# Gate projections of a two-layer mixer as three products of rounded parts, their sigmoids moved to a later stage

## The chip, the core and the metric

One core of a Trainium2 chip runs the whole program. The metric is device microseconds of one execution; the number given for a kernel is the median over its runs.

## What is computed

The reference is a long block on 256 tokens of width 1024. Two layers of a first block come first (feed-forward, mixer, feed-forward), then a second block with a recurrent part and 32 experts. The change touches only the mixer of the two layers. In short:

```
h      = rms_norm(x, mix_norm[l])
q,k,v  = split(h @ w_in[l])                       # four kinds of attention, a b c d
y_a .. y_d = attention of each kind               # a: 4 heads of 128, b c d: 4 heads of 64
gate   = sigmoid(h @ w_gate[l] + b_gate[l])       # 4 x 1024 columns, one block of 1024 for each branch
mixed  = sum over br of gate_br * (y_br @ w_br)   # br = a, b, c, d
x      = x + mixed @ w_out[l]
```

## The kernel before

Activations lie transposed: 8 blocks of 128 features by 256 tokens. The weights stream from HBM through a ring of three slots `RB` (`load_ring`, L388), each filled by one transfer of up to 2 MB; a slot is filled again when the step named in its job is done (for the gates the last of its four products, L353).

Most matrix products of the kernel are made of rounded parts. A weight w becomes wh, its value rounded to the format float32r by ScalarE (a Copy, `Split.high`, L417), and wl = w - wh by VectorE (`Split.low`, L426). The activations are split in the same way. A product is then the sum of three float32r products wl*xh + wh*xl + wh*xh (`mm3`, L279). The gate projections are not made so: they are plain float32 products of `HA` (the normalised x) and the raw slot (L970).

A mixer has three stages, one after the other. Every engine waits between them (`everyone`).

- `project` (L787) makes q, k, v in ten groups and at its end writes the normalised x into `HA` (L864).
- `attend` (L891) is the attention. First 12 turns of q and k on TensorE, evicted by ScalarE and VectorE in equal parts (L1036, L1100). Then one list, `attention_order()` (L159), gives the order of everything else on all three engines. Its entries are (kind, head, phase) or ("gate", h, 0) for h from 0 to 31. Each engine walks the same list and does its share of each entry.
- `branches` (L1221) makes y_br @ w_br from rounded parts, VectorE multiplies each product by its gate (L1287), GpSimd adds them up (L1308), and w_out follows.

The list begins, with one round in each line (s is a step of the top-k mask for kind d, n a step of the norm of kind a, and "c0.1" is phase 1 of head 0 of kind c):

```
c0.0 s.0 gate0
c0.1 c1.0 s.1 gate1 gate2
c0.2 c1.1 c2.0 s.2 gate3
c0.3 c1.2 c2.1 s.3 gate4
c1.3 c2.2 c3.0 s.4 gate5 gate6
c2.3 c3.1 a0.0 s.5 gate7
c3.2 a0.1 a1.0 s.6 gate8
c3.3 a0.2 a1.1 s.7 gate9 gate10
a0.3 a1.2 a2.0 s.8 gate11
a1.3 a2.1 a3.0 s.9 gate12
a2.2 a3.1 b0.0 s.10 gate13 gate14
a2.3 a3.2 b0.1 s.11 gate15
a3.3 b0.2 b1.0 s.12 gate16
...
b3.3 gate23
d0.0 n.0 gate24 gate25
d0.1 d1.0 n.1 gate26 gate27
d0.2 d1.1 d2.0 n.2 gate28 gate29
d0.3 d1.2 d2.1 gate30 gate31
d1.3 d2.2 d3.0
d2.3 d3.1
d3.2
d3.3
```

For a head of kind a, b or d: phase 0 is the logits on TensorE; phase 1 (`soften`, L1132) is on VectorE the row maxima (L1143), then the exponentials on ScalarE (L1064), then the division and mixing on VectorE (L1156 to L1170); phase 2 is three transposes on TensorE (L1004), which wait for phase 1, and their copy by ScalarE (L1070); phase 3 is the product with v (L1022) and its copy by VectorE (L1130). For kind c: phase 1 is the masked logits on VectorE (L1119), Abs, Exp and Ln on ScalarE (L1075 to L1079) and one step of VectorE (L1121); phase 2 is a product on TensorE that waits for it (L1015), an addition on VectorE (L1126) and an Exp on ScalarE (L1083); phase 3 is as above. Step n.2 has the square roots (L603), two reciprocals (L607) and four scalings (L1213).

A gate before: TensorE makes 8 float32 products of 128 x 256 (L969), and ScalarE evicts them as Sigmoid with the bias into `SG`, a part of `kept` (L1044). VectorE does nothing at a gate and walks past it.

## Time and profile before

| what | value |
|---|---|
| median of 3 runs | 2796.01 us (2793.53 to 2804.36) |
| the profiled execution: its own time | 2803.41 us |
| the profiled execution: its span | 2801.5 us |
| mean granted TensorE clock | 0.942 of full speed |
| TensorE matmul busy | 2551.5 us (91%) |
| VectorE busy | 1442.3 us (51%) |
| ScalarE busy | 1195.9 us (43%) |
| attention stage of layer 0 | 350 to 527 us of the span |
| attention stage of layer 1 | 1132 to 1308 us of the span |

The span goes from the first to the last instruction; the execution's own time adds what lies around it. PE is TensorE's matmuls and PEld its weight loads, DVE is VectorE, ACT is ScalarE, POOL is GpSimd and SPq the queue that issues the transfers. A row such as "0.71 <-DVE AT L1121" in square brackets gives the idle time of the engine just before the instruction, and what ended it. The tile names in the rows are those of the program: `AT` is the work area of the attention stage, `kept` holds q, k, v, the gates and the branch inputs, `ps` is PSUM, `mpwh`, `mpwl`, `mbwh`, `mbwl` are rounded parts of weights in the stages before and after.

### The profile page before, as it was taken

The page shows a single profiled execution, that of the slowest core. Times are in us where ns is not written, and L with a number is a line of the kernel's source. Part 1 is how long each engine was busy: PE and PEld are TensorE (multiplying, and loading weights), DVE is VectorE, ACT ScalarE, POOL GpSimd, SP SyncE. Part 2 cuts the span into 40 slices and gives each one's busy share as a digit, 9 for nine tenths or more (in the row PEclk, how much of TensorE's full clock was granted, in tenths as well). Part 3 has the DMA queues.
Part 4 walks back from the last instruction along what each step waited for, and adds up shares of the span by engine and source line. Part 5 has one row for each costly group of instructions (what it writes and reads, how often), then busy time and mean ns, then how long its engine had stood idle before and what let it go on. Part 6 is the DMA issues. An engine that isn't in the chain of part 4 may idle for free.

```text
span 2801.5 us, 52642 instructions
## 1 busy us (share of the span) xinstructions
PE 2551.5 (91%) x23295; PEld 2190.1 (78%) x23295; DVE 1442.3 (51%) x2249; ACT 1195.9 (43%) x1723; POOL 299.1 (11%) x425
## 2 busy tenths in 40 slices
PE   7999899889999999998899987787978889989997
PEld 7997788779999988787799955664467778868786
DVE  5654533566556545344665553342435442168885
ACT  5333374444344333654443452221244432157773
POOL 0100000121001000000310000531123222000000
PEclk9999999999999999999999988797979999989999
DMA  7653513347547534222466221001100002449993
GB/s 238 231 197 135 184 61 120 106 151 241 196 154 238 196 136 170 104 91 105 163 218 228 87 90 61 3 3 35 61 32 4 4 4 95 150 148 366 361 363 129
DMA packets 268885, 396.09 MB, mean 141 GB/s; under 512 B 9320, under 2 KB 172829, under 8 KB 268525
## 3 DMA queue, kind: packets, MB, share of 16 engines
q1 hardware_dynamic: 266921, 389.25, 40.6%
q8 instruction: 186, 3.05, 0.5%
q0 software_dynamic: 1120, 2.17, 0.3%
q10 hardware_dynamic: 612, 1.24, 0.1%
q14 instruction: 46, 0.38, 0.0%
HBM read 391.59 MB, written 1.05 MB: 140 GB/s over the span
## 4 chain that ended last, share of the span: by engine, by line
PE 37%; DVE 8%; DMA 5%; issue 5%; ACT 3%; POOL 2%; SPq 0%; DVEq 0%; POOLq 0%; ACTq 0%
PE ps L277 36%; DMA RB<-in_moe_w_up 5%; DVE gwl L426 2%; ACT gwh L417 1%; PE ps L499 1%; POOL H L1308 1%; DVE AR L1729 0%; POOL AR L1935 0%; POOL AR L2308 0%; DVE AR L607 0%; DVE AR L1475 0%; DVE AR L1537 0%; DVE AR L2016 0%; ACT L2514 0%; POOL AR L1471 0%
## 5 line engine op out<-in xcount | busy, mean ns | idle before, releaser
L277 PE MATMUL ps<-H,RB 128*128 128x256 f32 (+1 forms) x1712 | 454.8, 423 | 10.3 <-issue 9.1
L277 PEld LDWEIGHTS ps<-H,RB 128*128 128x128 f32 x1712 | 325.6, 193 | 124.1 <-issue 86.1
L426 DVE TENSOR_TENSOR wl<-RB,wh 128x2048 fp32r<-128x2048 f32 (+1 forms) x136 | 302.9, 2230 | 207.8 <-ACT wh L417 207.3
L277 PE MATMUL ps<-xh,wl 128*128 128x256 f32 x1408 | 402.5, 286 | 0.0
L277 PE MATMUL ps<-xl,wh 128*128 128x256 f32 x1408 | 399.2, 284 | 0.0
L277 PE MATMUL ps<-xh,wh 128*128 128x256 f32 x1408 | 399.2, 284 | 0.0
L277 PE MATMUL ps<-AR 64*64 64x64 f32 (+3 forms) x8296 | 314.6, 244 | 56.1 <-issue 18.3
L277 PEld LDWEIGHTS ps<-AR 64*64 64x64 f32 (+1 forms) x8296 | 262.5, 148 | 112.3 <-issue 82.8
L417 ACT ACTIVATE wh<-RB 128x2048 fp32r<-128x2048 f32 (+1 forms) x136 | 251.6, 1853 | 161.3 <-PE ps L277 122.9
L277 PEld LDWEIGHTS ps<-xh,wl 128*128 128x128 f32 x1408 | 271.1, 193 | 10.2 <-issue 10.1
L277 PEld LDWEIGHTS ps<-xl,wh 128*128 128x128 f32 x1408 | 271.2, 193 | 0.1
L277 PEld LDWEIGHTS ps<-xh,wh 128*128 128x128 f32 x1408 | 271.0, 192 | 0.0
L426 DVE TENSOR_TENSOR gwl<-RB,gwh 128x2048 fp32r<-128x2048 f32 x96 | 217.4, 2290 | 39.8 <-ACT gwh L417 38.9
L417 ACT ACTIVATE gwh<-RB 128x2048 fp32r<-128x2048 f32 x96 | 183.1, 1917 | 56.1 <-DMA RB<-in_moe_w_up 32.7
L277 PE MATMUL ps<-hh,wl 128*128 128x256 f32 x704 | 199.2, 283 | 0.0
L277 PE MATMUL ps<-hl,wh 128*128 128x256 f32 x704 | 199.2, 283 | 0.0
L277 PE MATMUL ps<-hh,wh 128*128 128x256 f32 x704 | 199.2, 283 | 0.0
L713 ACT ACTIVATE H<-H 128x256 f32<-128x256 f32 x88 | 36.8, 418 | 307.4 <-DVE H L740 307.4
L277 PEld LDWEIGHTS ps<-hh,wl 128*128 128x128 f32 x704 | 135.2, 192 | 0.0
L277 PEld LDWEIGHTS ps<-hl,wh 128*128 128x128 f32 x704 | 135.2, 192 | 0.0
L277 PEld LDWEIGHTS ps<-hh,wh 128*128 128x128 f32 x704 | 135.2, 192 | 0.0
L1308 POOL TENSOR_TENSOR H<-H 128x256 f32<-128x256 f32 x48 | 46.2, 1002 | 761.6 <-DVE H L1287 761.6
(415 smaller groups left out, 4522.1 us busy)
## 6 DMA issues: line engine op xcount, KB each, us to landing
RB<-in_ffn_w_gu SPq DMA_DIRECT2D x88, 1024.0 KB, 7.6
RB<-in_w_in SPq DMA_DIRECT2D x25, 2048.0 KB, 7.7
RB<-in_ffn_w_down SPq DMA_DIRECT2D x16, 2048.0 KB, 7.9
RB<-in_w_gate SPq DMA_DIRECT2D x16, 2048.0 KB, 8.8
RB<-in_moe_w_gate SPq DMA_DIRECT2D x32, 1024.0 KB, 7.6
RB<-in_moe_w_up SPq DMA_DIRECT2D x32, 1024.0 KB, 10.2
RB<-in_moe_w_down SPq DMA_DIRECT2D x32, 1024.0 KB, 8.5
RB<-in_ada_w SPq DMA_DIRECT2D x12, 2048.0 KB, 11.0
```

The lines of the kernel that those rows point to most:

```text
L277: return M.matmul(o, lhsT, rhs, start=start, stop=stop, skip_group_check=True)
L417: S.activation(self.pair(h)[0], of(slot_of(*key)), ACT.Copy).then_inc(*did("high", self.name, h))
L426: V.tensor_tensor(lo, of(slot_of(*key)), hi.bitcast(F32), ALU.subtract).then_inc(*did("low", self.name, h))
L499: ins = M.transpose(ps[0:s.shape[1], 128 * i:128 * i + s.shape[0]], s, ident[0:s.shape[0], 0:s.shape[0]])
L713: S.activation(sil[:, n % 4, 0, :], sil[:, n % 4, 0, :], ACT.Silu).then_inc(*did("silu", f, n))
L1308: P.tensor_tensor(HB[:, c, :], HB[:, c, :], tmp[:, ((br - 1) * 8 + c) % 4, :], ALU.add).then_inc(*did("merged", l, br, c))
```

## The change

The gates become products of rounded parts, like the other projections.

- ScalarE rounds the weights of a gate, 128 x 1024, into one of three buffers (two from gate 24 on, as the third lies where the last gates are written). VectorE writes the rest back in place into the ring's slot. Both are done by a new class `GateWeights`: gates 0 and 1 within `project`, gate 2 ahead of the list, and at gate h of the list, behind its eviction, the weights of gate h + 3.
- The normalised x is split as well: 8 Copies of ScalarE at the end of `project`, 8 subtractions of VectorE at the start of `attend`, ahead of its other work.
- TensorE makes 24 float32r products for a gate in place of 8 float32 ones.
- The eviction is Identity with the bias, in place of Sigmoid. The sigmoids are taken in `branches`, for a branch at once (128 x 2048, in place in `SG`).

The program's own areas move by 8 columns, and `SM` is 4 columns shorter. The transfers, their slots and what frees them stay as they were.

```diff
@@ -75,12 +75,12 @@
     pe_once="lam cum ab route ranks cw glo wide_c spread", eg="dg", ed="dd", columns="merge mgate out2 conv shift z",
     rw_in="w_in ic_in cums bon_in k_in", gdn_in="re_gate cumg wide_g kk kb_t",
     act_once="lam_exp sine f_log g_log beta group_exp expert_exp lnx_root o_root sil w2 low_act xd_high",
-    rows="k_rows v_rows rv_rows o_rows u_rows back ob b_rows k_rows_r", h_high="d_high", h_silu="d_silu",
+    rows="k_rows v_rows rv_rows o_rows u_rows back ob b_rows k_rows_r", h_high="d_high gw_high u_high", h_silu="d_silu",
     padded="shift_pad", conv_silu="z_silu", copied_a="out_a x_in_a ctx_a", part_high="m_high y_high",
-    gdn_exp="exp_c exp_d exp_g exp_tot", gdn_copy="kb_neg v_out", merge_a="yb mgated", rw_act="w_sig ic exps",
+    gdn_exp="exp_c exp_d exp_g exp_tot", gdn_copy="kb_neg v_out", merge_a="yb mgated", rw_act="opened w_sig ic exps",
     dve_once="lam_dot lam_diff nlam angle by_row dup f_in soft_f iw cq eps blk decay g_in mod scl o_square o_gated "
              "renorm_sq lnx_square a2 logits group_in expert_in combined rank known chosen cw_out cb_t xd_low",
-    copied_v="x_in ctx_v out_v vec", h_low="d_low", h_scaled="c_scaled d_scaled", part_low="m_low y_low", taps="moved",
+    copied_v="x_in ctx_v out_v vec", h_low="d_low", h_scaled="c_scaled d_scaled gw_low u_low", part_low="m_low y_low", taps="moved",
     unit_k="unit_kk kk_in", gdn_v="neg_a beta_g cumg_out qk_dec q_dec g64 d_in", pad_zero="shift_zero g2 sil_zero", gdn_mask="masked_e masked_l",
     gdn_rows="kb k_dec", inv_0="inv_own", rw_v="bt kt pr bon e1l both").items() for name in names.split()}

@@ -153,7 +153,7 @@

 BASE = 16512
 O_CST, O_RB, O_XT, O_H, O_VEC, O_SM = 0, 3912, 16200, 18248, 22344, 22728
-STAGE = 24032
+STAGE = 24024


 def attention_order():
@@ -229,8 +229,11 @@
         RB = sb("RB", O_RB, [NSLOT, 4096])
         XT = sb("XT", O_XT, [KD, T])
         H = sb("H", O_H, [2, KD * T])
+
+        RBR = sb("RBR", O_RB, [NSLOT, 4096], F32R)
+        HR = sb("HR", O_H, [2, KD, T], F32R)
         VEC = sb("VEC", O_VEC, [3, 128])
-        SM = sb("SM", O_SM, [1300])
+        SM = sb("SM", O_SM, [1296])
         HA = H[:, 0, :].rearrange("p (k n) -> p k n", k=KD)
         HB = H[:, 1, :].rearrange("p (k n) -> p k n", k=KD)
         RST = SM[:, 144:400]
@@ -780,11 +783,46 @@
             kept = sb(f"kept{l}", STAGE, [13312])
             PQK, SG = view(kept, 0, 2, NK), view(kept, 0, 32, T)
             VN, YT = view(kept, 8192, 2, 1280), view(kept, 10752, 10, T)
-            project(l, PQK, VN, view(kept, 10752, 1024))
-            attend(l, PQK, SG, VN, YT)
+            gw = GateWeights(l, [sb(f"GW{l}", STAGE + 27136, [2, 1024], F32R)[:, i] for i in range(2)]
+                             + [sb(f"GX{l}", STAGE + 7168, [1024], F32R)])
+            project(l, PQK, VN, view(kept, 10752, 1024), gw)
+            attend(l, PQK, SG, VN, YT, gw)
             branches(l, SG, YT)

-        def project(l, PQK, VN, TMP):
+        class GateWeights:
+
+
+
+            def __init__(self, l, bufs):
+                self.l, self.bufs, self.n = l, bufs, [0, 0]
+                self.of = [h % 3 if h < 24 else h % 2 for h in range(32)]
+                self.last = [max((x for x in range(h) if self.of[x] == self.of[h]), default=None) for h in range(32)]
+
+            def parts(self, h):
+                i, j = divmod(h, 4)
+                slot = job_no["gate", self.l, i] % NSLOT
+                w, lo = (x[:, slot, :].rearrange("p (k n) -> p k n", k=KD)[:, :, 128 * j:128 * j + 128] for x in (RB, RBR))
+                return self.bufs[self.of[h]].rearrange("p (k n) -> p k n", k=KD), w, lo
+
+            def high(self, upto_gate):
+                while self.n[0] < min(upto_gate, 32):
+                    h = self.n[0]
+                    hi, w, _ = self.parts(h)
+                    AC.wait_ge(*landed("gate", self.l, h // 4))
+                    if self.last[h] is not None:
+                        AC.wait_ge(*at("gate", self.l, self.last[h]))
+                    S.activation(hi, w, ACT.Copy).then_inc(*did("gw_high", self.l, h))
+                    self.n[0] += 1
+
+            def low(self, upto_gate):
+                while self.n[1] < min(upto_gate, 32):
+                    h = self.n[1]
+                    hi, w, lo = self.parts(h)
+                    DV.wait_ge(*at("gw_high", self.l, h))
+                    V.tensor_tensor(lo, w, hi.bitcast(F32), ALU.subtract).then_inc(*did("gw_low", self.l, h))
+                    self.n[1] += 1
+
+        def project(l, PQK, VN, TMP, gw):
             st, g = f"p{l}", R_MX + 8 * l
             o = STAGE + 13312
             wh, wl = sb(f"mpwh{l}", o, [2, 2048], F32R), sb(f"mpwl{l}", o + 4096, [2, 2048], F32R)
@@ -837,12 +875,17 @@
                 scaled_act(st, g, xh)
                 for gi in range(len(GROUPS)):
                     ws.high(2 * gi + 3)
+                    if gi == len(GROUPS) - 1:
+                        gw.high(2)
                     AC.wait_ge(*at("proj", l, gi, 1))
                     AC.wait_ge(*at("by_row", l))
                     for s, lo, hi in evictor(gi, 1)[1]:
                         ins = S.activation(out_of(s, lo, hi, 1), ps_of("proj", l, gi, 1, 1)[:, lo - GROUPS[gi][0]:hi - GROUPS[gi][0]],
                                            ACT.Copy, scale=by_row[:, 1:2])
                     ins.then_inc(*did("seg_a", l, gi))
+                for k in range(KD):
+                    AC.wait_ge(*at("normed", l, k))
+                    S.activation(HR[:, 1, k, :], HA[:, k, :], ACT.Copy).then_inc(*did("u_high", l, k))

             def vector():
                 ws.low(1)
@@ -854,6 +897,8 @@
                 DV.wait_ge(*at("by_row", l))
                 for gi in range(len(GROUPS)):
                     ws.low(2 * gi + 3)
+                    if gi == len(GROUPS) - 1:
+                        gw.low(2)
                     DV.wait_ge(*at("proj", l, gi, 1))
                     for s, lo, hi in evictor(gi, 0)[1]:
                         ins = V.tensor_scalar(out_of(s, lo, hi, 0), ps_of("proj", l, gi, 1, 0)[:, lo - GROUPS[gi][0]:hi - GROUPS[gi][0]],
@@ -888,7 +933,7 @@
             vector()
             everyone(("seg_v", l, 9), ("seg_a", l, 9), ("rot", l, AT["diq"], 1), ("normed", l, 7))

-        def attend(l, PQK, SG, VN, YT):
+        def attend(l, PQK, SG, VN, YT, gw):
             ar = sb(f"AT{l}", STAGE + 13312, [13824])
             QKT = view(ar, 0, 25, T)
             EB, PTB = view(ar, 6400, 8, 384), view(ar, 9472, 8, 384)
@@ -962,12 +1007,13 @@
                 PE.wait_ge(*at("qk_v", l, 22))
                 for kind, h, phase in order:
                     if kind == "gate":
-                        i, j = divmod(h, 4)
-                        sv = slot_of("gate", l, i).rearrange("p (k n) -> p k n", k=KD)
-                        PE.wait_ge(*landed("gate", l, i))
+                        hi, _, lo = gw.parts(h)
+                        PE.wait_ge(*at("gw_low", l, h))
                         ps = bank(("gate", l, h), ("gated", l, h))
                         for k in range(KD):
-                            ins = mm(ps[:, 0:T], sv[:, k, 128 * j:128 * j + 128], HA[:, k, :], k == 0, k == KD - 1)
+                            PE.wait_ge(*at("u_low", l, k))
+                            ins = mm3(ps[:, 0:T], (hi[:, k, :], lo[:, k, :]),
+                                      (HR[:, 1, k, :], HR[:, 0, k, :]), k == 0, k == KD - 1)
                         ins.then_inc(*did("gate", l, h))
                     elif kind == "score" and phase < 8:
                         q = QKT[64 * (phase % 2):64 * (phase % 2) + 64, 20 + phase // 2, :]
@@ -1038,11 +1084,13 @@

                 AC.wait_ge(*at("turned", l, "ik"))
                 AC.wait_ge(*at("iw", l))
+                gw.high(3)
                 for kind, h, phase in order:
                     if kind == "gate":
                         AC.wait_ge(*at("gate", l, h))
-                        S.activation(SG[:, h, :], ps_of("gate", l, h)[:, 0:T], ACT.Sigmoid,
+                        S.activation(SG[:, h, :], ps_of("gate", l, h)[:, 0:T], ACT.Identity,
                                      bias=vec(R_BG + 32 * l + h)).then_inc(*did("gated", l, h))
+                        gw.high(h + 4)
                     elif kind == "score" and phase < 8:
                         before_e(AC, "score", phase)
                         AC.wait_ge(*at("logit", l, "score", phase))
@@ -1083,6 +1131,10 @@
                         S.activation(PT("c", h), E("c", h, 0), ACT.Exp).then_inc(*did("stuck", l, h))

             def vector():
+                for k in range(KD):
+                    DV.wait_ge(*at("u_high", l, k))
+                    V.tensor_tensor(HR[:, 0, k, :], HA[:, k, :], HR[:, 1, k, :].bitcast(F32), ALU.subtract).then_inc(
+                        *did("u_low", l, k))
                 for i in range(2):
                     ins = V.tensor_copy(DUP[:, :, 64 * i:64 * i + 64], PQK[:, :, AT["dik"]:AT["dik"] + 64])
                 ins.then_inc(*did("dup", l))
@@ -1104,8 +1156,11 @@
                 DV.wait_ge(*at("cum", l))
                 V.tensor_scalar(ST[:, 32:40], ps_of("cum", l)[:, 0:8], -1.0, None, ALU.mult).then_inc(*did("cq", l))
                 DV.wait_ge(*at("cq", l))
+                gw.low(3)
                 for kind, h, phase in order:
-                    if kind == "score":
+                    if kind == "gate":
+                        gw.low(h + 4)
+                    elif kind == "score":
                         score(phase)
                     elif kind == "normalise" and phase == 2:
                         normalise()
@@ -1259,10 +1314,19 @@
                                   (yh[:, k, :], yl[:, k, :]), k == 0, k == KD - 1)
                     ins.then_inc(*did("out", l, c))

+            def opened(b):
+
+                sg = SG[:, 8 * b:8 * b + 8, :].rearrange("p a n -> p (a n)")
+                S.activation(sg, sg, ACT.Sigmoid).then_inc(*did("opened", l, b))
+
             def scalar():
                 ws.high(1)
                 for c in range(10):
                     S.activation(yh[:, c, :], YT[:, c, :], ACT.Copy).then_inc(*did("y_high", l, c))
+                ws.high(2)
+                for b in range(4):
+                    opened(b)
+                    ws.high(b + 3)
                 ws.high(8)
                 AC.wait_ge(*at("branch", l, 3, 7))
                 for c in range(KD):
@@ -1283,6 +1347,7 @@
                         DV.wait_ge(*at("branch", l, br, c))
                         if br and n_t >= 4:
                             DV.wait_ge(*at("merged", l, *divmod(n_t - 4 + 8, 8)))
+                        DV.wait_ge(*at("opened", l, br))
                         dst = tmp[:, n_t % 4, :] if br else HB[:, c, :]
                         V.tensor_tensor(dst, ps_of("branch", l, br, c)[:, 0:T], SG[:, 8 * br + c, :], ALU.mult).then_inc(
                             *did("weighted", l, br, c))
```

## Rows read from the trace of the kernel before

**Rows 1.** Busy time by stretch, layer 0 (us, then busy and instructions of each engine, granted clock).

```profile
342.00:346.00 4.00, 4.00 (x20) 4.00 (x20) 0.00 (x0) 0.00 (x0) 0.00 (x0) 0.57 0.84 279
...
362.00:406.00 44.00, 43.29 (x219) 34.81 (x218) 12.75 (x37) 34.45 (x48) 0.00 (x0) 1.00 0.21 73
406.00:480.00 74.00, 73.65 (x359) 59.42 (x358) 34.46 (x158) 41.62 (x86) 0.00 (x0) 1.00 0.27 99
480.00:521.00 41.00, 40.13 (x188) 32.36 (x186) 14.24 (x37) 21.24 (x38) 0.00 (x0) 1.00 0.35 124
```

**Rows 2.** Groups of instructions by line and shape in 345 to 520 us.

```profile
L277 PE MATMUL ps<-H,RB 128*128 128x256 f32 x512 | 115.5, 382 | 0.0
L1044 ACT ACT_TABLE_LOAD x17 | 21.8, 1283 | 0.3
```

**Rows 3.** Timeline of ScalarE: the evictions of two gates that follow each other.

```profile
475.26 0.47 ACT L1044 ACTIVATE kept<-ps,VEC 128x256 f32<-128x256 f32 x1 [2.91 <-PE ps L277]
478.71 0.47 ACT L1044 ACTIVATE kept<-ps,VEC 128x256 f32<-128x256 f32 x1 [2.98 <-PE ps L277]
```

**Rows 4.** Timeline of VectorE in `branches`: evictions of w_out's products, each 24 float32r matmuls of 128x256.

```profile
595.37 0.42 DVE L1299 TENSOR_TENSOR XT<-XT,ps 128x256 f32<-128x256 f32 x1 [2.46 <-PE ps L277]
598.25 0.42 DVE L1299 TENSOR_TENSOR XT<-XT,ps 128x256 f32<-128x256 f32 x1 [2.45 <-PE ps L277]
```

**Rows 5.** Timelines of ScalarE and VectorE outside the stage: splitting of weights and activations.

```profile
551.57 1.06 ACT L417 ACTIVATE mbwh<-RB 128x1024 fp32r<-128x1024 f32 x1 [3.91 <-PE ps L277]
...
553.78 1.33 DVE L426 TENSOR_TENSOR mbwl<-RB,mbwh 128x1024 fp32r<-128x1024 f32 x1
...
340.14 1.39 DVE L426 TENSOR_TENSOR mpwl<-RB,mpwh 128x1184 fp32r<-128x1184 f32 x1
...
531.13 3.44 DVE L1277 TENSOR_TENSOR mbyl<-kept,mbyh 128x256 fp32r<-128x256 f32 x10
```

**Rows 6.** Timeline of VectorE: the last copy ahead of the list.

```profile
359.00 0.42 DVE L1103 COPY AT<-ps 128x256 f32<-128x256 f32 x1
```

**Rows 7.** Timeline of one round of kind c, all engines.

```profile
375.56 0.51 ACT L1075 ACTIVATE AT<-AT 128x384 f32<-128x384 f32 x1
375.61 3.72 PE L277 MATMUL ps<-H,RB 128*128 128x256 f32 x16
...
378.36 0.47 ACT L1049 ACTIVATE AT<-ps 128x384 f32<-128x384 f32 x1
...
380.17 0.41 DVE L1130 COPY kept<-ps 64x256 f32<-64x256 f32 x1 [0.46 <-PE ps L277]
...
381.71 0.55 DVE L1119 TENSOR_TENSOR AT<-ps,CST 128x384 f32<-128x384 f32 x1
...
381.98 3.72 PE L277 MATMUL ps<-H,RB 128*128 128x256 f32 x16
```

**Rows 8.** Timeline of VectorE: the first and the last step of phase 1 of a head of kind a.

```profile
424.23 0.28 DVE L1143 CUSTOM_DVE_ANT_0 AT<-ps,CST 128x128 f32<-128x128 f32 x1
...
427.92 0.75 DVE L1168 SCALAR_TENSOR_TENSOR AT<-AT,SM 128x128 f32<-128x128 f32 x2
```

**Rows 9.** Timeline of TensorE: its two waits within the list, and the end of gate 31.

```profile
402.21 1.11 PE L277 MATMUL ps<-AT,CST 128*128 128x256 f32 x6 [0.71 <-DVE AT L1121]
...
428.72 0.55 PE L1004 MATMUL ps<-CST,AT 128*128 128x128 f32 x3 [0.35 <-DVE AT L1168]
...
517.14 0.86 PE L277 MATMUL ps<-AT,kept 128*64 128x256 f32 x4
```

**Rows 10.** Timeline of VectorE in step n.2.

```profile
506.00 6.57 DVE L607 RECIPROCAL AT<-AT 128x512 f32<-128x512 f32 x2 [1.25 <-ACT AT L603]
```

**Rows 11.** Timeline of TensorE at a wait near the end of `project`.

```profile
341.58 0.40 PE L277 MATMUL ps<-mpwh,mpxl 128*128 128x296 f32 x1 [1.80 <-DVE mpwl L426]
```

**Rows 12.** Two lines of the second block, an Ln and an Exp that follow each other.

```profile
L1663 ACT ACT_TABLE_LOAD  x1: 1283/1283/1283, 1652.0 to 1652.0; - x1
...
L1664 ACT ACT_TABLE_LOAD  x1: 1283/1283/1283, 1653.5 to 1653.5; - x1
```

## The prediction, made before the changed kernel was run

> **What bounds the kernel now.** I read the busy time by stretch first. From 362 to 521 us TensorE is busy nearly all the time, at full clock, while VectorE is busy for a third to a half and ScalarE for half to three quarters [rows 1]. The groups by line then show what fills TensorE: the gate products alone are 115.5 of these 160 us, and ScalarE loads its function table 17 times for the Sigmoid [rows 2]. The timeline of TensorE shows only two waits within the list [rows 9]. Layer 1 repeats layer 0 in the same views, so all below is worked out for one layer and doubled.
>
> The reader should see one more thing in the timeline of VectorE and ScalarE: these engines are not free when TensorE needs them. TensorE's two waits, 0.71 and 0.35 us, are for VectorE [rows 9]. The round of kind c in the rows takes TensorE 6.37 us from one gate to the next (375.61 to 381.98), and within it ScalarE's Abs, Exp and Ln take 2.80 us up to the next step (375.56 to 378.36) [rows 7]. So a shorter gate makes TensorE wait soon, and each microsecond put on the chain that goes through VectorE is seen.
>
> **TensorE's part.** Two evictions of gates that follow each other are 3.45 us apart, so a gate is 3.45 us [rows 3]. A product of w_out is what a new gate will be, 24 float32r matmuls of the same shape, and its evictions are 2.88 us apart [rows 4]. 0.57 us less for each gate, 32 gates: **-18.2 us** for a layer, if TensorE stays the bound.
>
> **What is added, and where it stands.** The Copy of a gate's weights is 1.06 us, the subtraction 1.22 us by my choice: 1.33 us is the row of the same shape, but GpSimd was at work beside it; the row of 1184 columns, 1.39 us, times 1024/1184 gives 1.20 [rows 5]. The bounds are 1.20 and 1.33. For 32 gates that is 34 us of ScalarE and 39 us of VectorE. ScalarE gets back the Sigmoid's 17 loads, 21.8 us [rows 2], and some of the loads for Exp behind them. By busy time both fit. By order they don't:
>
> - VectorE did nothing at a gate and walked on to the next maxima. Now it waits at gate h for the Copy of gate h + 3, which ScalarE issues behind the eviction of gate h. After TensorE ends a gate it takes 0.47 + 1.06 + 1.22 = **2.75 us** before VectorE can touch what stands behind it in the list. Queued behind it are the maxima, the masks of kind c and the copies of y; ScalarE's Exps wait for those, VectorE again for the Exps, and TensorE's transposes (phase 2) for the result.
> - From gate 24 on there are two buffers, so the Copy of gate h + 3 also waits for gate h + 1.
>
> Start of the stage: VectorE's 8 subtractions stand ahead of everything. Ten took 3.44 us [rows 5], so 2.75. They delay the input of kind b's forget gate, its Exp and Ln, and all six evictions behind these, of which the last copy ended at 359.42 [rows 6]. Part of it was slack, as the evictions waited a little for TensorE's turns; I take **+2.0** (bounds 1.0 and 2.75). Gates 0 and 1 are split while both engines wait in `project`: nothing; uncovered it would be 2 us.
>
> Kind c, gates 0 to 7. In a round with one gate ScalarE and VectorE now work in series: 2.75, copy of y 0.41, two additions of 0.55, Abs to Ln 2.80, Relu 0.47, in sum 7.5 us. TensorE's round becomes 6.37 - 0.57 = 5.8. Through the eight rounds, where those with two gates give time back, I get waits of about 1.5 us ahead of c1.2, c2.2 and c3.2: **+4.6**, less the 0.71 there was.
>
> Kind a, gates 8 to 15. Phase 1 took 4.44 us (424.23 to 428.67) [rows 8]. In a one-gate round VectorE has 1.22 + 0.41 + 4.44 + 1.3 for the step s = 7.4 us, TensorE about 5.5. Rounds with two gates, and the one without phase 1, absorb some. Waits: 1.2 at a0.2, 2.7 at a2.2, 1.1 at b0.2: **+5.0**, less 0.35.
>
> Kind b, gates 16 to 23. Phase 1 has one map instead of two, some 3.0 us (an estimate from the 4.44), and TensorE has the longer logits. It keeps up and stays the bound but for 1.0 at b3.2: **+1.0**. Here the gates pay.
>
> Kind d, gates 24 to 31. Behind gate 26: Copy and subtraction for gate 28 (2.3), phase 1 of d0 (3.0), against 2.88 for gate 27: TensorE waits 2.4. Behind gate 28: Copy and subtraction for gate 30 (2.3), phase 1 of d1 (3.0), the square roots (1.2), the two reciprocals 6.57 [rows 10], the scalings (1.8) and only then the subtraction of gate 31 (1.2), in sum 16.1 us. Meanwhile TensorE has gates 29 and 30 and a few small products, 8.3 us with a wait of 1.6 at d1.2. It then waits 7.8. Together **+11.8**. This is the largest single cost: the reciprocals were hidden, since no TensorE work before gate 31's end at 517.14 hung on them [rows 9].
>
> The last heads of d hang on VectorE as before: nothing. In `branches` the four sigmoids (about 1.9 us each) fall into ScalarE's waits for TensorE (3.91 us ahead of one Copy [rows 5]), the first ends as VectorE comes to need it: **+0.1**; if the gaps were gone, 7.6. The transfers of gates have some 20 us of slack, and in-place subtraction frees slots where they were freed: nothing.
>
> Clock: behind a wait of 1.80 us [rows 11], which came soon after a shorter one, the granted clock fell to 0.57 for 4 us [rows 1], which is half speed nearly throughout and cost about 1.8 us. Behind 7.8 us idle I count it once for each layer, partly covered by VectorE's work for d2: **+1.0**.
>
> Sum for a layer: 2.0 - 18.2 + 3.9 + 4.65 + 1.0 + 11.8 + 0.1 + 1.0 = **+6.2**; for both +12.4. The durations come from the profiled execution, of 2803.41 us with a span of 2801.5, 7.4 us above the median of the runs; 2803.4 would become 2815.8. The difference is added to the median, 2796.0: **2808 us**.
>
> **A rule weighed.** In the second block an Exp directly behind an Ln has a load of its own, 1.28 us [rows 12], so I keep one load for Exp and one for Ln in each head of kind c. The Trainium skill (ScalarE: Activation LUTs, "Table sets: the hidden batching unit") says that one set holds both exp and ln, and that a load between them is saved. By it the Ln of three waiting heads would come 1.28 us sooner, 7.7 us for both layers, and the sum would be 2801. The trace disagrees with it for this build.
>
> **Rivals.**
> - *TensorE stays the bound* (faster). For it speak the busy sums of the other engines [rows 1]. The gates' 36.4 us would be had less 4 for the start: 2764. Against it: the trace already shows TensorE waiting for VectorE with the longer gate. Milder: the added waits, 22.4 us a layer, are half as long: 22 us back, 2786. It ends at faster by over 0.5% only if they are under some 40% of mine.
> - *The clock falls behind the short waits too* (slower). There are nine waits a layer of 1 to 3 us. At 1.8 us a fall, as in [rows 1], five more falls a layer where TensorE then is the bound give +18: 2826. From one more fall in a layer on it decides for slower by over 0.5%. For it: the fall behind 1.80 us. Against: of the two waits of the list neither was followed by one, though both were short, and where VectorE is the bound a slow TensorE costs less.
> - *Exp and Ln share a table once no Sigmoid stands between*: 2801, against the rows.
>
> **Chances.** Forecast 0.55, TensorE the bound 0.05, half waits 0.15, clock 0.2, shared table 0.05. No change within 0.5% (14 us: 2782 to 2810) is about what a measurement of this kernel can tell. Faster: 0.05 and under half of 0.15: 0.11. Slower: the clock's 0.2 and some 0.35 of the forecast's 0.55: 0.39. Same: 0.50. The range goes from the half waits to the clock's case: 2785 to 2826. The likeliest case alone has 2799 to 2817, by the bounds of start, subtraction and waits.
>
> **What the profile after would show.** Gate evictions in a row 2.9 us apart; no table load at the evictions. TensorE idle ahead of c1.2, c2.2, c3.2 for the step behind Ln, ahead of a2.2 for phase 1, and ahead of gate 31 for a subtraction, 5 to 9 us. VectorE's idle time before the gates' subtractions, ended by ScalarE. The last gate's end later than before relative to the stage's start, by 2 to 6 us, while gate 23's is earlier by 1 to 4. What would make me wrong: VectorE not held up at the gates, gate 31's parts ready before the reciprocals, or a granted clock below 0.9 through the list.

## The result and the profile after

The changed kernel takes **2825.42 us** (median of 5 runs, 2816.12 to 2830.30) against 2796.01 us before: a ratio of 1.0096, with a 95% interval of 1.0069 to 1.0123. In a second set of runs, told below, it was 1.0092 (1.0072 to 1.0112). So it is slower by about 0.9%, where I had forecast 2808 us, 0.4% slower. It is inside my range, close to its upper end, and it is the number of my rival "the clock falls behind the short waits too" (2826 us, chance 0.2). That it meets the rival to within 1 us is partly luck: the second set's median is 2818.85.

The page of the profiled execution (2830.3 us) has these totals: span, then busy time and instructions of each engine.

```profile
span 2828.6 us, 53826 instructions
...
PE 2538.9 (90%) x23807; PEld 2203.1 (78%) x23807; DVE 1523.6 (54%) x2329; ACT 1205.1 (43%) x1757; POOL 299.8 (11%) x425
```

TensorE is busy 12.6 us less than the 2551.5 before, and the span is 27.1 us longer. The comparison that tells most is that of the whole attention stage, from TensorE's first turn to its first product of `branches`. Here it is in the windows view, for the kernel before, layers 0 and 1 (columns as in [rows 1]: length, busy time of PE, PEld, DVE, ACT and POOL, then the granted clock; the last two are the DMA engines' share and GB/s):

```profile
350.02:531.69 181.67, 171.12 (x836) 138.93 (x837) 70.92 (x255) 110.97 (x199) 0.00 (x0) 0.96 0.25 87
1131.69:1313.36 181.67, 171.11 (x837) 138.93 (x837) 70.92 (x254) 110.97 (x199) 0.00 (x0) 0.96 0.25 88
```

and for the changed kernel:

```profile
347.06:539.65 192.59, 159.18 (x1093) 140.52 (x1093) 108.81 (x293) 101.83 (x201) 0.00 (x0) 0.93 0.24 83
1139.00:1333.53 194.53, 162.61 (x1092) 144.05 (x1093) 108.73 (x293) 101.93 (x201) 0.00 (x0) 0.90 0.23 82
```

The stage is 10.9 us longer in layer 0 and 12.9 in layer 1. TensorE's busy time is lower (171.1 to 159.2 and 162.6), so the products did become cheaper. Its idle time, the length less the busy time, went from 10.6 us to 33.4 and 31.9. And the granted clock went from 0.96 to 0.93 and 0.90. The stretches of layer 0 that [rows 1] shows at full clock are now (the last one 1 us shorter):

```profile
362.00:406.00 44.00, 37.52 (x270) 32.79 (x269) 21.20 (x39) 32.69 (x47) 0.00 (x0) 0.99 0.21 70
406.00:480.00 74.00, 68.40 (x495) 60.92 (x495) 52.16 (x177) 36.30 (x88) 0.00 (x0) 0.98 0.29 102
480.00:520.00 40.00, 29.82 (x210) 26.77 (x208) 18.41 (x31) 16.57 (x31) 0.00 (x0) 0.96 0.29 105
```

Where TensorE now waits is seen in its timeline, layer 0. [rows 9] has the two waits, 0.71 and 0.35 us, that it had before between the gates. (Shown are the waits over 1.4 us up to gate 31.)

```profile
380.21 1.11 PE L280 MATMUL ps<-AT,CST 128*128 128x256 f32 x6 [1.71 <-DVE AT L1176]
...
429.14 0.55 PE L1050 MATMUL ps<-CST,AT 128*128 128x128 f32 x3 [2.92 <-DVE AT L1223]
...
499.07 0.52 PE L1050 MATMUL ps<-CST,AT 128*128 128x128 f32 x3 [2.42 <-DVE AT L1218]
...
508.06 0.36 PE L280 MATMUL ps<-HR,RBR 128*128 128x256 f32 x1 [3.05 <-DVE SM L1198]
...
520.70 0.58 PE L280 MATMUL ps<-HR,RBR 128*128 128x256 f32 x1 [5.34 <-DVE RBR L822]
```

All are ended by VectorE: a step of kind c's chain (L1176), the probabilities of a2 (L1223) and of d0 (L1218), the maxima of d1, which free a PSUM bank (L1198), and the subtraction of a gate's weights (L822). The view of the clock (after POOL's 0.00) behind three of these waits:

```profile
430.00:436.00 6.00, 6.00 (x32) 5.41 (x32) 4.89 (x20) 2.08 (x9) 0.00 (x0) 0.72 0.00 1
499.00:504.00 5.00, 4.93 (x24) 4.14 (x25) 1.23 (x1) 0.81 (x2) 0.00 (x0) 0.66 0.92 371
520.00:524.00 4.00, 3.30 (x17) 3.30 (x17) 2.41 (x10) 1.34 (x5) 0.00 (x0) 0.57 0.01 4
```

In the trace's record of the granted clock these are stretches at 1.2 GHz: 431.5 to 434.9, 499.7 to 503.2 and 520.2 to 523.6 us; a fourth is 359.8 to 363.2, behind the first waits of the stage. TensorE is busy in nearly all of these stretches, and its products start 0.21 us apart in them (521.50, 521.72) where they start 0.12 us apart at full clock (509.19, 509.31). So each costs it about half its length, 1.7 us. No fall came at once behind the waits of 1.71 and 3.05 us.

Before there was none of these stretches up to gate 31. But the list has one more wait there that neither the rows nor the prediction show, behind the last gate, ahead of d3.2, and behind it the clock was at 1.2 GHz for 13.7 us (523.2 to 536.9), partly beyond the stage. The timeline of TensorE and the windows view of the kernel before:

```profile
523.28 0.87 PE L1004 MATMUL ps<-CST,AT 128*128 128x128 f32 x3 [3.16 <-DVE AT L1163]
...
523.20:531.70 8.50, 2.42 (x8) 1.28 (x8) 3.21 (x4) 5.31 (x12) 0.00 (x0) 0.50 0.00 0
```

### The profile page after: what moved, and what is told of

Its sections match the earlier page's. It is cut to its first block, busy times and chain, and to the rows that moved or that the text cites. A ratio compares the mean times of both kernels' runs of the same rounds, so it can differ in the third digit from the quotient of the medians.

```text
span 2828.6 us, 53826 instructions
## 1 busy us (share of the span) xinstructions
PE 2538.9 (90%) x23807; PEld 2203.1 (78%) x23807; DVE 1523.6 (54%) x2329; ACT 1205.1 (43%) x1757; POOL 299.8 (11%) x425
## 3 DMA queue, kind: packets, MB, share of 16 engines
HBM read 391.59 MB, written 1.05 MB: 139 GB/s over the span
## 4 chain that ended last, share of the span: by engine, by line
PE 67%; DVE 12%; ACT 7%; issue 6%; DMA 5%; POOL 2%; SPq 0%; ACTq 0%; DVEq 0%; POOLq 0%
PE ps L280 66%; DMA RB<-in_moe_w_up 5%; DVE gwl L429 2%; POOL H L1373 1%; ACT gwh L420 1%; DVE RBR L822 1%; ACT GW L814 1%; DVE mpwl L429 1%; DVE AR L1794 0%; ACT AT L1112 0%; DVE AT L610 0%; POOL AR L2373 0%; ACT wh L420 0%; DVE AR L610 0%; DVE AR L1540 0%
## 5 line engine op out<-in xcount | busy, mean ns | idle before, releaser
L280 PE MATMUL ps<-AR 64*64 64x64 f32 (+3 forms) x8296 | 322.6, 248 | 52.5 <-issue 17.3
L280 PEld LDWEIGHTS ps<-AR 64*64 64x64 f32 (+1 forms) x8296 | 269.0, 152 | 111.1 <-issue 83.5
L280 PE MATMUL ps<-H,RB 128*128 128x256 f32 (+1 forms) x688 | 224.3, 486 | 10.3 <-issue 9.1
L280 PEld LDWEIGHTS ps<-H,RB 128*128 128x128 f32 x688 | 134.7, 198 | 92.1 <-issue 78.5
L280 PE MATMUL ps<-HR,RBR 128*128 128x256 f32 x512 | 155.8, 304 | 19.6 <-DVE RBR L822 9.3
L280 PE MATMUL ps<-HR,GW 128*128 128x256 f32 x768 | 150.6, 298 | 0.0
```

The lines of the kernel that those rows point to most:

```text
L280: return M.matmul(o, lhsT, rhs, start=start, stop=stop, skip_group_check=True)
```

## The experiments

The kernels were run in three sets, each on one chip beside the kernel before (medians there 2796.89, 2794.54 and 2794.07 us). Ratios are to that kernel. The table has, for layer 0 / layer 1 of each profiled execution, the length of the stage as above, TensorE's idle time in it and the time that the clock stood at 1.2 GHz (from the trace's record).

```
kernel                        median   ratio (95% interval)       stage           idle          at 1.2 GHz
before                       2796.01   -                          181.7 / 181.7   10.6 / 10.6   14.4 / 14.4
changed                      2825.42   1.0096 (1.0069, 1.0123)    192.6 / 194.5   33.4 / 31.9   28.7 / 37.5
changed_again                2818.85   1.0092 (1.0072, 1.0112)    195.1 / 196.0   32.3 / 31.9   38.1 / 39.0
one_product                  2771.56   0.9919 (0.9893, 0.9946)    169.8 / 173.3   54.4 / 49.5   77.6 / 94.8
sigmoids_only                2790.03   0.9972 (0.9960, 0.9984)    179.3 / 180.3    9.9 /  9.9   12.1 / 13.1
low_one_gate_later           2805.51   1.0031 (1.0019, 1.0042)    184.3 / 184.5   22.7 / 22.6   34.1 / 34.3
norm_after_d2                2815.78   1.0066 (1.0043, 1.0089)    191.6 / 194.7   31.8 / 31.4   34.6 / 41.1
split_x_early                2815.74   1.0083 (1.0061, 1.0105)    190.8 / 191.4   31.0 / 31.1   30.4 / 31.0
kind_d_reordered             2796.29   1.0005 (0.9991, 1.0019)    185.4 / 180.6   25.3 / 24.9   31.8 / 20.2
all_reordered                2769.28   0.9911 (0.9895, 0.9927)    167.7 / 167.3   15.0 / 15.1   14.1 / 13.7
waits_filled                 2811.02   1.0053 (1.0032, 1.0074)    188.3 / 187.5   17.9 / 17.9   17.6 / 16.9
gates_own_banks              2825.98   1.0109 (1.0089, 1.0129)    198.3 / 197.9   30.4 / 29.9   48.1 / 47.8
reordered_sigmoid_in_place   2788.96   0.9977 (0.9962, 0.9993)    178.3 / 177.9   23.5 / 23.2   21.3 / 20.8
```

The median less the two stages is 2428 to 2438 us in all thirteen rows. The stages are those of the one profiled execution; that execution's own time less its stages is 2422 to 2443 us. So most of what the kernels differ by is in these two stages, and the rest of the program scatters, by up to some 20 us from one execution to another.

### The changed kernel again

No edit; it runs beside the second set.

> The changed kernel once more, unaltered. Theory A: the 7 us that its profile shows in the untouched second block is chance, that of how the stretches at half clock fall there; another profile of the same program has another length there, between 1400 and 1420 us from the last feed-forward's start to the end, and the two attention stages again 11 to 13 us longer than before. Rival: the second block is longer because of the change (moved areas, more instructions): again 1420 us. The median stays at 2820 to 2830 us in either case.

Measured: 2818.85 us, ratio 1.0092. The slowdown repeats. In the first profile the program behind the second mixer took 6 us longer than before (1428.0 against 1421.6 us); here it took 10 less than before (1411.2). The change does not touch that part, and as it went both ways I put it down to chance. TensorE's idle time is that of the first profile or 1.1 us less, yet the clock was low for 9.4 us more in layer 0: with nearly the same waits, the number of falls varies from one execution to the next.

### What bounds the stage: one product in place of three

```diff
-                            ins = mm3(ps[:, 0:T], (hi[:, k, :], lo[:, k, :]),
-                                      (HR[:, 1, k, :], HR[:, 0, k, :]), k == 0, k == KD - 1)
+                            ins = mm(ps[:, 0:T], hi[:, k, :], HR[:, 1, k, :], k == 0, k == KD - 1)
```

> The changed kernel with only the product wh*xh of each gate (8 float32r matmuls in place of 24; the two products with the low parts are left out, all splitting and all waits stay). Theory A, the chain ScalarE - VectorE behind each gate sets the pace in kinds c, a and d: most of the 1.9 us x 64 = 121 us that TensorE loses turns into waiting; only kind b and the rounds with two gates get shorter, some 15 us a layer: about 2795 us. Rival B, TensorE's work is still the bound: 2825 - 121 = 2705 us. Rival C, the granted clock: with TensorE idle more often it falls more often, and the time stays above 2800.

Measured: 2771.56 us. Two thirds of the gates' products are gone, 32 x 1.88 = 60 us of TensorE in a layer (by the 2.82 us of a gate), and the stage is only 21 to 23 us shorter. TensorE waits in its place; the longest entries of its waits, 345 to 545 us (total, times, longest):

```profile
PE ps L1049 <- DVE AT L1217: 16.2, 6, 3.7
...
PE ps L280 <- DVE AT L1175: 9.4, 3, 4.6
PE ps L1049 <- DVE AT L1222: 7.4, 3, 4.8
PE ps L280 <- DVE RBR L822: 5.8, 2, 5.5
```

So behind TensorE's gate products stands a chain through VectorE and ScalarE, with TensorE's short products at the low clock in it, that is only some 20 us shorter than the changed stage. It gives more than theory A had (2795): of the 60 us a layer a third was still on the path, although TensorE waited far more and the clock was low for half of the stage.

### The sigmoids alone

The kernel before, with the eviction as a plain sum and the sigmoids of a branch in `branches`.

```diff
-                        S.activation(SG[:, h, :], ps_of("gate", l, h)[:, 0:T], ACT.Sigmoid,
+                        S.activation(SG[:, h, :], ps_of("gate", l, h)[:, 0:T], ACT.Identity,
```

> The kernel before with one part of the change alone: float32 gate products, evicted with Identity, the sigmoids of a branch at once in the later stage. Theory A: TensorE was the bound, so 17 table loads fewer on ScalarE in a layer give back only the 1.06 us of waits of TensorE; 2792 to 2798 us, with four sigmoids hidden in the later stage. Rival: the four sigmoids (7.6 us a layer) are on the path of the later stage: 2811 us. Rival: the table loads were what TensorE waited for: 2785 us.

Measured: 2790.03 us, 7 us faster than before and below theory A's range. ScalarE's busy time in the stage fell from 110.97 to 74.61 us, TensorE's idle time only from 10.6 to 9.9. The stage is 1.4 to 2.4 us shorter, as TensorE was the bound; the rest of the 7 us lies outside the two stages or is scatter. This part of the change is no loss.

### VectorE's subtraction one gate later

At gate h of the list VectorE waits for the Copy of gate h + 3, just issued. Here it does gate h + 2's, whose Copy is long done.

```diff
-                        gw.low(h + 4)
+                        gw.low(h + 3 if h < 23 else h + 4)
```

> The changed kernel, with VectorE subtracting the weights of gate h + 2 at gate h in place of those of gate h + 3, up to gate 22: it no longer waits for the eviction and the Copy that follow gate h. Theory A: the 1.5 us (0.47 + 1.06) at each gate leave the chain; the waits ahead of c0.2 to c3.2, a0.2, a2.2, b0.2 shrink from about 13 us a layer to 5: 2809 us, and the waits in kind d stay. Rival (the subtraction's own 1.23 us or the bank that is free too late is what counts, not the wait): 2820 to 2825 us.

Measured: 2805.51 us, 13 to 20 us less than the changed kernel, which ran in the other sets (0.6% by the ratios), and 10.7 us less idle time of TensorE in layer 0. Theory A had 2809. Its waits for the probabilities of kind a went from 2.9 to 1.2 us and those for kind c's step from 4.4 to 1.4. Ahead of the subtractions for gates 0 to 24 VectorE waited 2.6 us for the Copies in layer 0, where it waited 20.6 in the changed kernel. No instruction was taken away: it is the place in VectorE's list that cost this. The clock was low for as long as in the changed kernel (34 us a stage), so what came back here are the waits.

### The reciprocals behind d2

```diff
-                    elif kind == "normalise" and phase == 2:
-                        normalise()
...
+                        if (kind, h) == ("d", 2):
+                            normalise()
```

> The changed kernel, with VectorE doing the norm of kind a (two reciprocals, 6.6 us, four scalings) behind phase 1 of head d2 in place of ahead of the subtraction for gate 31. Theory A: TensorE's wait of 5.3 us ahead of gate 31 goes, but VectorE is late for y of d1 and phase 1 of d3; net 2 to 3 us a layer: 2820 us. Rival: the wait ahead of gate 31 was fully on the path and the tail has room: -5 us a layer, 2815 us. Rival: the tail pays it all back: 2825 us.

Measured: 2815.78 us, 3 to 10 us less than the changed kernel (0.3% by the ratios, with overlapping intervals). That is the number of the first rival and not its mechanism, as the tail had no room. The wait of gate 31 is gone, and the last head waits in its place, in TensorE's timeline:

```profile
533.29 0.87 PE L1050 MATMUL ps<-CST,AT 128*128 128x128 f32 x3 [7.09 <-DVE AT L1218]
534.80 1.54 PE L280 MATMUL ps<-AT,kept 128*64 128x256 f32 x4 [0.64 <-ACT AT L1118]
```

Before and after the change the first of these waits was 3.2 us; the reciprocals stand ahead of d3's probabilities now. Moved as one piece the 6.6 us only hit someone else.

### The split of x earlier

The 8 Copies and 8 subtractions for x stand in the last group of `project`, ahead of the end of the stage.

```diff
+                        for k in range(KD):
+                            AC.wait_ge(*at("normed", l, k))
+                            S.activation(HR[:, 1, k, :], HA[:, k, :], ACT.Copy).then_inc(*did("u_high", l, k))
...
+                        for k in range(KD):
+                            DV.wait_ge(*at("u_high", l, k))
+                            V.tensor_tensor(HR[:, 0, k, :], HA[:, k, :], HR[:, 1, k, :].bitcast(F32), ALU.subtract).then_inc(
```

> The changed kernel, with the normalised x split within the last group of the projection stage, where both engines wait, in place of at the start of the attention stage. Theory A: the 2.0 us that I gave to the start of a stage come back: 2821 us. Rival (the start is hidden behind the turns): no change, 2825 us.

Measured: 2815.74 us, 3.1 below the changed kernel of the same set, which the two intervals don't tell apart. It fits with the start's 1.3 us a layer.

### Kind d reordered

From gate 23 on the subtractions are one gate later, one reciprocal stands behind gate 28's weights, the other behind d2's phase 1, and the scalings behind d3's.

```diff
-                        gw.low(h + 4)
+                        gw.low(h + 4 if h < 23 else h + 3)
+                        if h == 28:
+                            normal_root(0)
...
+                        if (kind, h) == ("d", 2):
+                            normal_root(1)
+                        elif (kind, h) == ("d", 3):
+                            normalise()
```

> The changed kernel, with the last part of VectorE's list reordered: from gate 23 on the subtraction at gate h is for gate h + 2, one reciprocal of the norm stands behind gate 28, the other behind phase 1 of d2, the scalings behind phase 1 of d3. Theory A: TensorE's waits ahead of d0.2 (2.4), gate 29 (3.05, for a PSUM bank that the maxima of d1 free late) and gate 31 (5.3) go but for about 1 us: -9 us a layer, 2807 us. Rival (the tail pays it back, as VectorE sets the pace there): above 2818 us.

Measured: 2796.29 us, 22.6 less than the changed kernel of the same set, 11 less than theory A, and level with before. Idle time fell by 7 us a stage, which alone would be 14. The two layers of its profile show what comes on top, in the windows view:

```profile
347.73:533.14 185.41, 160.09 (x1092) 140.89 (x1093) 108.60 (x293) 101.84 (x201) 0.00 (x0) 0.91 0.24 86
1133.13:1313.74 180.61, 155.74 (x1092) 137.72 (x1093) 108.61 (x293) 101.65 (x201) 0.00 (x0) 0.94 0.25 89
```

The same instructions and nearly the same idle time (25.3 and 24.9 us), but 31.8 and 20.2 us at 1.2 GHz, and 185.4 and 180.6 us of stage. Here 11.6 us of low clock cost 4.8 us.

### All of it reordered

The split of x early, the subtractions one gate later everywhere, and kind d as above.

> Both reorderings and the later subtraction at all gates together: VectorE no longer waits for the eviction at a gate, x is split early, kind d reordered. Theory A: the parts add up, -20 (as measured for the later subtraction) -18 -4: 2783 us, faster than the kernel before (2797). Rival (VectorE's own work of 39 us a layer keeps it the pace-setter in kind a, and the clock falls stay): 2795 us or more.

Measured: **2769.28 us, ratio 0.9911 (0.9895 to 0.9927)**: it beats both kernels, and theory A's 2783. The stage:

```profile
349.95:517.64 167.69, 152.73 (x1092) 135.25 (x1093) 105.20 (x285) 102.28 (x201) 0.00 (x0) 0.96 0.27 95
1118.83:1286.13 167.30, 152.25 (x1093) 134.76 (x1093) 105.24 (x285) 102.26 (x201) 0.00 (x0) 0.96 0.27 95
```

It is 14.0 and 14.4 us shorter than before, with the clock as before. Within the list one wait over 1.1 us is left; it and the tail's:

```profile
495.08 0.86 PE L280 MATMUL ps<-AT,kept 128*64 128x256 f32 x4 [1.57 <-ACT AT L606]
...
509.25 0.85 PE L1054 MATMUL ps<-CST,AT 128*128 128x128 f32 x3 [3.61 <-DVE AT L1222]
```

(The first is for ScalarE's square roots; the tail's was 3.2 us before.) VectorE waits for the Copies of gate weights 11.1 us in layer 0 where it waited 40.1 us in the changed kernel. This is as much work on each engine as in the changed kernel, in another order. The clock fell nowhere in the list up to gate 31, and of the 20 us a layer that the cheaper gates are worth 14 are had: TensorE's busy time is 18.4 us below that of the kernel before, its idle time 4.4 above.

### The waits filled

The test of the clock: ahead of nine steps TensorE makes products of constants, into the bank that it is about to write, so that it is busy and gets the same work done at the same time. (At gate 31 it claims the bank ahead of its wait for the weights, and no longer behind it.)

```diff
+            fills = {("c", 0): 1, ("c", 1): 3, ("c", 2): 3, ("c", 3): 1, ("a", 2): 6, ("b", 0): 3, ("b", 3): 2,
+                     ("d", 0): 5, ("gate", 31): 10}
+
+            def fill(ps, kind, h):
+                for _ in range(fills.get((kind, h), 0)):
+                    mm(ps[:, 0:256], ident, cst(C_CAUS, 256), True, True)
```

> The changed kernel, with TensorE doing extra float32 products of constants (0.43 us each) in eight of its waits: 1 ahead of c0.2, 3 ahead of c1.2 and c2.2, 1 ahead of c3.2, 6 ahead of a2.2, 3 ahead of b0.2, 2 ahead of b3.2, 5 ahead of d0.2, 10 ahead of gate 31. They go into the PSUM bank that the next product overwrites, and fill some four fifths of each wait. Theory A: it is TensorE's idle time in these waits that makes its granted clock fall, and the falls cost 8 to 10 us a layer: the half-clock time in a stage drops from 30 to 46 us to about 20 (22.6 and 19.2 in the kernel before), and the time by 10 to 20 us, to some 2805 us, although TensorE does more work. Rival (the falls come with the float32r products or with chance): half-clock time unchanged and 2820 us or more.

Measured: 2811.02 us, 8 us below changed_again and 14 below the first runs of the changed kernel, though in other sets of runs; by the ratios, 0.4% both times. (The expectation counts the low clock over a longer stretch than my table does.) TensorE's timeline where the wait ahead of a2.2 was 2.92 us:

```profile
425.90 2.75 PE L280 MATMUL ps<-CST 128*128 128x256 f32 x12
428.99 0.55 PE L1059 MATMUL ps<-CST,AT 128*128 128x128 f32 x3 [0.33 <-DVE AT L1233]
```

The transposes come at 428.99 in place of 429.14: the fill delays nothing. And the stage:

```profile
346.98:535.24 188.26, 170.36 (x1160) 148.59 (x1161) 108.70 (x293) 101.79 (x201) 0.00 (x0) 0.95 0.24 85
1135.38:1322.91 187.53, 169.64 (x1160) 147.97 (x1161) 108.66 (x293) 101.76 (x201) 0.00 (x0) 0.96 0.24 85
```

The time at 1.2 GHz is 17.6 and 16.9 us against 28.7 to 39.0 in the four stages of the changed kernel, and the stage is 4 to 9 us shorter. Of the falls between the first gate and gate 31, four to six a layer in the two profiles of the changed kernel, only the one behind the start is left, in both layers; that wait was not filled. Only more work was issued. So the falls come from the idle time, and this part of the slowdown is the clock's. Yet not every wait brings one: the one of 2.96 us ahead of gate 29 was not filled either, and no fall followed it. The stage of the kernel before is still 6 us shorter: that is the waits themselves, less what the cheaper gates give.

### Banks of their own for the gates

The gates get PSUM banks 6 and 7, everything else 0 to 5, against the waits of gates 7, 8 and 29 for banks that maxima and kind c's step free late.

```diff
-                        ps = bank(("gate", l, h), ("gated", l, h))
+                        ps = bank(("gate", l, h), ("gated", l, h), among=(6, 7))
```

> The changed kernel, with two PSUM banks for the gates alone and six for all else in the attention stage. Theory A: gate 29 waits 3.05 us for a bank that the maxima of d1 free, gates 7 and 8 wait 1.34 and 0.78 us likewise; with own banks these waits go, but the next step (d1.2, c3.2, a0.2) waits for the same VectorE work a little later: 2 us a layer, 2816 to 2821 us. Rival: the full 5.2 us a layer come back: 2812 us. Rival: two banks are too few and gates wait for their own evictions: 2825 us or more.

Measured: 2825.98 us, ratio 1.0109. That is the number of the last rival. The wait for L1198 is gone and others are longer; TensorE idles 2 us less than in changed_again, but the clock is low for 9 to 10 us more, and the stage is 2 to 3 us longer. From TensorE's waits, 345 to 545 us:

```profile
PE ps L1050 <- DVE AT L1218: 9.7, 5, 3.2
...
PE ps L280 <- ACT kept L1091: 1.6, 1, 1.6
```

The second line is a gate that waits for the eviction of the gate two before it, the last rival's mechanism, but it is one wait of 1.6 us. So banks of their own don't help: the VectorE work behind them is late, and TensorE meets it one step later.

### The reordered kernel with its sigmoids back in place

all_reordered, with Sigmoid at the eviction and none in `branches`.

```diff
-                        S.activation(SG[:, h, :], ps_of("gate", l, h)[:, 0:T], ACT.Identity,
+                        S.activation(SG[:, h, :], ps_of("gate", l, h)[:, 0:T], ACT.Sigmoid,
```

> The reordered kernel (2769 us) with the other part of the change undone: each gate evicted as Sigmoid, no sigmoids in the later stage. Theory A: once ScalarE's chain sets the pace in kind c, the table loads of 1.28 us matter more than in the kernel before, where the moved sigmoids gave 7 us: 2785 to 2795 us. Rival: with VectorE freed of its wait the loads are hidden: 2765 to 2775 us.

Measured: 2788.96 us, 20 us above all_reordered and within theory A. The loads of the function table are back, in both layers together:

```profile
L1095 ACT ACT_TABLE_LOAD x34 | 43.6, 1283 | 0.6
...
L1116 ACT ACT_TABLE_LOAD x22 | 28.2, 1283 | 0.4
```

L1095 is the eviction, L1116 kind a, b and d's Exp, which has 2 loads in all_reordered. The same edit was worth 7 us in the kernel before and is worth 20 here: TensorE idles 8 us more a stage (23.5 and 23.2 against 15.0 and 15.1) and the clock is low for 7 us more. That ScalarE's Copies and evictions are now on the way of VectorE and TensorE is my reading of it.

## Why it is 2825 and not 2808

By the terms of the prediction, for layer 0, in us:

```
term                      predicted   measured
start                       +2.0        +1.3    first product behind the turns 10.73 us after the first turn; 9.45 before
gates                      -18.2       -20.2    32 x (3.45 - 2.82)
kind c, less the 0.71       +3.9        +5.0    0.80 + 1.71 + 1.37 + 1.34 + 0.48 - 0.71
kind a, less the 0.35       +4.65       +4.7    0.78 + 2.92 + 1.39 - 0.35
kind b                      +1.0        +1.3    1.30 at b3.2
kind d                     +11.8       +10.8    2.42 + 3.05 + 5.34
branches                    +0.1         0      TensorE idles 9.1 us from its first to its last product there, in both
clock                       +1.0        +8.3    busy time fell 11.9 and not 20.2
sum                         +6.2       +11.2    the stage: +10.9
```

The clock's term is what is left of TensorE's busy time; half of the 14.3 us that the low clock lasted longer would be 7.2.

**The step that failed is the clock's.** I counted one fall a layer, behind gate 31, and priced it 1.0. In layer 0 there were four more falls than before, in layer 1 five, two of them twice as long, and the low clock lasted 23.1 us longer; half of that is 11.6 us, and TensorE's busy time is 11.7 above what cheaper gates alone would give (171.1 - 20.2 = 150.9 against 162.6). Together 20.0 us where I had 2.0; cheaper gates, the start and shorter waits in layer 1 (a slow TensorE waits less) gave back 6.6. I had the price of a fall about right ([rows 1]: 1.8; here 1.7) and their number wrong, since I took the two short waits of [rows 9], which no fall followed, as a guide for waits of 1.7 to 3 us. The nearer rows were [rows 11] with the 0.57 of [rows 1], and the 3.16 us ahead of d3.2 with the low clock behind it, which I left out: it is not so that the list had only two waits. The rival had the mechanism. Its number, five falls a layer beside that of gate 31, was somewhat high for the count (four and five in all) and right for the cost (20.0 us in both layers, as measured), since two of the falls were longer. waits_filled shows that the waits cause them, and the two layers of kind_d_reordered what they cost.

The same shows in a sign that I had named. The eviction of gate 23 should have come 1 to 4 us earlier after the stage's start than before; it came 1.2 us later in both layers (134.3 against 133.1 us). That of gate 31 came 10.0 and 12.3 us later, where I had 2 to 6.

The Trainium skill (TensorE: Matmul & The Clock Gate, "A second HAM failure mode: psum-queue depth-cycling") tells of a kernel whose short idle times between groups of matmuls made the clock go up and down. This trace agrees: none of the waits within the list is longer than 5.34 us, most are under 3, and the clock fell 4 times in layer 0 between the first gate and gate 31. The same page of the Trainium skill ("HAM oscillation — how this bites in real kernels") prices time at the low clock at half its length; the two layers of kind_d_reordered give 0.41 (4.8 of 11.6 us), and TensorE's busy time in layer 1 of the changed kernel 0.51 (11.7 of 23.1).

**Gates.** 2.82 us and not 2.88, as shown by evictions at full clock in ScalarE's timeline:

```profile
436.42 0.47 ACT L1091 ACTIVATE kept<-ps,VEC 128x256 f32<-128x256 f32 x1 [2.23 <-PE ps L280]
...
439.24 0.47 ACT L1091 ACTIVATE kept<-ps,VEC 128x256 f32<-128x256 f32 x1 [1.40 <-PE ps L280]
```

**The waits.** Their sum came out (22.9 us for kinds c, a, b and d, against 22.4), their places in part. c1.2, c2.2, a2.2, b0.2, b3.2, d0.2 and gate 31 waited as said; c3.2 waited 0.48 us in place of some 1.5, c0.2 waited 0.80 unforeseen, and a0.2 did not wait. Gates 7, 8 and 29 waited for a PSUM bank that VectorE frees, which I had not seen; gate 29's 3.05 us stand in place of the 1.6 at d1.2, and shorten gate 31's wait. That was a hit by sum and not by place. Gate 31 waited 5.34 us, not 7.8, and its chain is as told, in VectorE's timeline:

```profile
511.17 6.56 DVE L610 RECIPROCAL AT<-AT 128x512 f32<-128x512 f32 x2 [1.25 <-ACT AT L606]
517.84 1.67 DVE L1268 SCALAR_TENSOR_TENSOR kept<-kept,SM,AT 128x256 f32<-128x256 f32 x4
519.43 1.21 DVE L822 TENSOR_TENSOR RBR<-RB,GW 128x1024 fp32r<-128x1024 f32 x1
```

The subtraction that gate 31 needs stands behind both reciprocals and the scalings. The mechanism at every gate is VectorE held up by a Copy that ScalarE issues just before. It is in the same timeline, first ahead of the maxima of a2, for which TensorE then waits 2.92 us, and then in kind d, ahead of the maxima of d1:

```profile
423.18 1.23 DVE L822 TENSOR_TENSOR RBR<-RB,GX 128x1024 fp32r<-128x1024 f32 x1 [1.40 <-ACT GX L814]
...
506.13 1.23 DVE L822 TENSOR_TENSOR RBR<-RB,GW 128x1024 fp32r<-128x1024 f32 x1 [5.42 <-ACT GW L814]
```

The second is longer for another reason: from gate 24 on there are two buffers, so the Copy for gate 30 waits until TensorE has made gate 28, and VectorE with it. ScalarE's timeline:

```profile
505.04 1.06 ACT L814 ACTIVATE GW<-RB 128x1024 fp32r<-128x1024 f32 x1 [5.23 <-PE ps L280]
```

The prediction counts it so. What it misses is that gate 29 needs a bank that the maxima behind this subtraction free. low_one_gate_later takes the first away, kind_d_reordered the second together with the place of the reciprocals, whose parts are not told apart. The Copy took 1.05 us and the subtraction 1.23 (predicted 1.06 and 1.22).

**The other rivals.** "TensorE stays the bound" is refuted: one_product takes away 120 us of TensorE and gains 47 to 54, and TensorE idles 32 to 33 us in the stage of the changed kernel. "Exp and Ln share a table" is refuted for this build: in the changed kernel the Ln (L1127), which follows the Exp of L1125 directly, and the next Exp (L1131) each have a load of their own for every head of kind c, with no Sigmoid between (both layers):

```profile
L1127 ACT ACT_TABLE_LOAD x8 | 10.3, 1283 | 0.1
L1131 ACT ACT_TABLE_LOAD x8 | 10.3, 1283 | 0.1
```

**Both stages together** grew by 23.8 us, 11.4 more than predicted. The medians differ by 29.4 us in the first set, 5.6 more than these stages. In the second set they differ by 24.3, while the two stages of its profile grew by 27.7, so there 3.4 us are missing. What is left beyond the stages is in the part that the change doesn't touch; it was not settled further than that it goes both ways.

## What to carry to other kernels

An order written out by hand is balanced for the durations that it was written for: when TensorE's share of a step gets shorter and VectorE's longer, keep the work and look for where each new instruction stands. One whose input was issued just before it belongs one step later, and long ones without a user nearby go in pieces between the steps; here that turned 0.9% slower into 0.9% faster. When you count new waits of TensorE, add the low clock behind them; here it cost a third to a half of what the waits did.

## What the runs showed of the hardware

- Waits of 1.7 to 3.1 us with TensorE busy on both sides were followed by stretches at 1.2 GHz, though not each of them (28.7 to 39.0 us of such stretches in a stage, 14.4 before). Nearly the same waits gave 28.7 us in one execution and 38.1 in another. The wait of 3.05 us ahead of gate 29 had a fall behind it in layer 1 of the changed kernel and none in layer 0.
- Products without a use in these waits, 67 more matmul records a stage, made the kernel faster: 1.0053 of before in place of 1.0092, with the stage's granted clock at 0.95 and 0.96, where the changed kernel's first profile had 0.93 and 0.90.
- Fewer idle microseconds did not mean fewer falls: gates_own_banks idled 30.4 us against 32.3 and had 48.1 us at the low clock against 38.1.
- 24 float32r matmuls of 128x256 took 2.82 us at full clock, 8 float32 ones of the same shape 3.45: three products of rounded parts are 18% cheaper than one plain float32 product.
